# Three 256-column matmuls per weight block in the up groups of the MLPs, with ReLU and square on ScalarE

## The reference

```python
for i in range(DEPTH):                      # DEPTH = 2
    y = diff_attention(h, ...) if i % 2 == 0 else gla(h, ...)
    h = layer_norm(DN_ALPHA * h + y, ln_g[i, 0], ln_b[i, 0])
    f = squared_relu_mlp(h, mlp_w1[i], mlp_w2[i])
    h = layer_norm(DN_ALPHA * h + f, ln_g[i, 1], ln_b[i, 1])

def squared_relu_mlp(x, w1, w2):            # w1: 2048 x 8192, w2: 8192 x 2048
    return jnp.square(jax.nn.relu(x @ w1)) @ w2
```

## Time and profile before

| quantity | before |
|---|---|
| median of 3 runs | 2231.32 us |
| lowest, highest | 2231.12, 2233.16 us |
| span of the profiled execution, first to last instruction | 2231.0 us |
| TensorE (PE) busy | 99% of the span |
| VectorE (DVE), ScalarE (ACT) busy | 57%, 40% |
| mean granted TensorE clock | 0.997 of full speed |
| mean DMA rate | 187 GB/s |

### The profile page before, as it was taken

How to read it: one execution, slowest core, us unless ns; L and a number is a source line. 1 busy time by engine, 2 the same in 40 slices (tenths; PEclk the granted TensorE clock), 3 DMA queues, 4 the chain that set the end, 5 groups by cost and what they waited for, 6 DMA issues and landing times.

```text
span 2231.0 us, 28775 instructions
## 1 busy us (share of the span) xinstructions
PE 2208.7 (99%) x11312; PEld 1876.4 (84%) x11312; DVE 1262.0 (57%) x1074; ACT 897.8 (40%) x754; POOL 108.5 (5%) x94
## 2 busy tenths in 40 slices
PE   7999999999999999999999999999999999999998
PEld 6888888988888888888888888889888888888886
DVE  5555555854554464455676566668544645554555
ACT  4444443443343343343454344334434434433431
POOL 2000000300000000000020111102000000000000
PEclk9999999999999999999999999999999999999999
DMA  8545556654655554655446445647555546555542
GB/s 283 179 141 197 170 179 216 215 185 169 219 192 189 188 188 163 217 186 188 151 152 210 172 150 181 232 151 245 171 212 190 181 170 214 193 193 189 181 163 109
DMA packets 206592, 417.04 MB, mean 187 GB/s; under 512 B 6640, under 2 KB 6640, under 8 KB 205504
## 3 DMA queue, kind: packets, MB, share of 16 engines
q1 hardware_dynamic: 205056, 406.87, 53.4%
q0 software_dynamic: 1472, 9.25, 1.1%
HBM read 414.00 MB, written 2.10 MB: 187 GB/s over the span
## 4 chain that ended last, share of the span: by engine, by line
PE 98%; issue 0%; DMA 0%; DVE 0%; ACT 0%; POOLq 0%; POOL 0%; SPq 0%
PE ps L435 97%; PE ps L508 1%; DMA raw<-in_attn_w_qkv_dram 0%; PE ps L747 0%; PE ps L595 0%; DVE res L1233 0%; PE ps L576 0%; DVE res L1224 0%; ACT hi L782 0%; POOLq L89 0%; POOL ln_rstd L343 0%; SPq L291 0%; DVE ln_stats L1186 0%; DVE res L1060 0%; DVE ln_mean_var L1215 0%
## 5 line engine op out<-in xcount | busy, mean ns | idle before, releaser
L1040 DVE TENSOR_TENSOR lo<-raw,hi 128x2048 fp32r<-128x2048 f32 x384 | 882.0, 2303 | 582.9 <-ACT hi L782 582.8
L782 ACT ACTIVATE hi<-raw 128x2048 fp32r<-128x2048 f32 x384 | 734.5, 1917 | 929.4 <-PE ps L435 913.7
L435 PE MATMUL ps<-X,hi 128*128 128x512 f32 (+1 forms) x3008 | 994.3, 385 | 6.1 <-ACT hi L782 6.1
L435 PE MATMUL ps<-hi,F 128*128 128x512 f32 x2560 | 793.2, 390 | 0.0
L435 PE MATMUL ps<-X,lo 128*128 128x256 f32 x2816 | 769.5, 282 | 0.0
L435 PEld LDWEIGHTS ps<-X,hi 128*128 128x128 f32 x3008 | 553.4, 189 | 123.8 <-ACT hi L782 6.5
L435 PEld LDWEIGHTS ps<-hi,F 128*128 128x128 f32 x2560 | 480.5, 188 | 99.5
L435 PEld LDWEIGHTS ps<-X,lo 128*128 128x128 f32 x2816 | 530.1, 190 | 3.9
L435 PE MATMUL ps<-lo,F 128*128 128x512 f32 x1280 | 498.0, 389 | 0.0
L435 PEld LDWEIGHTS ps<-lo,F 128*128 128x128 f32 x1280 | 240.3, 188 | 49.5
L435 PE MATMUL ps<-hi,X 128*128 128x512 f32 x768 | 246.7, 396 | 0.0
(11 more groups left out here) (110 smaller groups left out, 528.0 us busy)
## 6 DMA issues: line engine op xcount, KB each, us to landing
raw<-in_mlp_w_dram SPq DMA_DIRECT2D x256, 1024.0 KB, 5.2
raw<-in_attn_w_qkv_dram SPq DMA_DIRECT2D x48, 1024.0 KB, 5.2
raw<-in_gla_w_in_dram SPq DMA_DIRECT2D x48, 1024.0 KB, 5.2
raw<-in_attn_w_o_dram SPq DMA_DIRECT2D x16, 1024.0 KB, 5.9
raw<-in_gla_w_o_dram SPq DMA_DIRECT2D x16, 1024.0 KB, 5.2
work<-in_ln_g_dram POOLq DMA_DIRECT2D x4, 1024.0 KB, 7.2
work<-in_ln_b_dram POOLq DMA_DIRECT2D x4, 1024.0 KB, 10.3
res<-in_x_dram SPq DMA_DIRECT2D x8, 256.0 KB, 11.1
```

The lines of the kernel that those rows point to most:

```text
L435: return pe.matmul(o, w, m, start=start, stop=stop)
L782: act.activation(hi[:, j], raw[:, j], ACT.Copy).then_inc(hi_ready, 1)
L1040: dve.tensor_tensor(lo[:, j], raw[:, j], hi[:, j].bitcast(F32), ALU.subtract).then_inc(lo_ready, 1)
```

## The change

In 15 of the 16 up groups of each MLP, `cols_group` is replaced by `up_group`. Each of the 64 weight blocks now gets three matmuls of 256 columns, all into one range of 256 PSUM columns: hi·X hi, hi·X lo, lo·X hi. The output blocks i share banks in pairs, so a group takes two banks (4·par and 4·par + 1) instead of four. Nothing is left to add: ScalarE reads both banks in one ReLU (128 x 1024), squares in place in a second instruction and later copies to F; VectorE only splits and writes the lo part of F, in one instruction of 1024 elements. There are two places for the hidden values, used in turn (`hidden`). The first up group of each MLP keeps `cols_by_block`, the copy and the add; it has windows of its own (`first_up_window`). Down groups, attention and GLA keep their instructions; some counters of `half_copied` change (`COPIED_MLP`, `COPIED_GLA`).

```diff
+        hidden = [part(5120, 4, SEQ), part(4096, 4, SEQ)]
@@ TensorE
-                    cols_group(g, 0, X)
+                    up_group(g, 0)
                 pe.wait_ge(res_added, 2 * r)
                 pe.wait_ge(halves_added, 2 * n)
-                cols_group(g + 1, 1, X)
+                up_group(g + 1, 1)
+
+            def up_group(g, par):
+
+                for j in range(TILES):
+                    pe.wait_ge(lo_ready, 4 * g + j + 1)
+                    for k in range(KPT):
+                        a = 4 * j + k
+                        first, last = a == 0, a == KT - 1
+                        for i in range(4):
+                            acc = ps[:, 4 * par + i // 2, (i % 2) * SEQ:(i % 2 + 1) * SEQ]
+                            mm(acc, hi[:, j, k, blk(i)], X[:, a, 0, :], first and i % 2 == 0, False)
+                            mm(acc, hi[:, j, k, blk(i)], X[:, a, 1, :], False, False)
+                            m = mm(acc, lo[:, j, k, blk(i)], X[:, a, 0, :], False, last and i % 2 == 1)
+                        if k == KPT - 1:
+                            m.then_inc(w_used, 1)
@@ ScalarE
+            def up_window(g, n, e, k, fk, hidden_free):
+
+                split_some(g + 1, 3)
+                act.wait_ge(w_used, 4 * g + 4)
+                act.wait_ge(*hidden_free)
+                act.activation(hidden[e].rearrange("p (b i) t -> p b (i t)", b=2), ps[:, 4 * e:4 * e + 2, :],
+                               ACT.Relu).then_inc(halves_added, 2)
+                act.wait_ge(halves_added, 2 * n + 2)
+                act.activation(hidden[e], hidden[e], ACT.Square).then_inc(squared, 2)
+                split_hi(g + 1, 3)
+                act.wait_ge(squared, k + 2)
+                act.activation(F[:, bass.ds(fk, 4), 0, :], hidden[e], ACT.Copy).then_inc(f_hi, 2)
...
@@ VectorE
+            def up_window(g, e, k, fk):
+                split_all(g + 1)
+                dve.wait_ge(f_hi, k + 2)
+                dve.tensor_tensor(F[:, bass.ds(fk, 4), 1, :], hidden[e], F[:, bass.ds(fk, 4), 0, :].bitcast(F32),
+                                  ALU.subtract).then_inc(f_lo, 2)
...
```

More of the change, by code:

```diff
@@ L74 @@
 COLS_GLA = 2 * PAIRS + 4 * CHUNKS
+COPIED_MLP = [2 * PAIRS, 2 * PAIRS + 5]
+COPIED_GLA = 2 * PAIRS + 1
 RES_MLP = [QUARTERS, 2 * QUARTERS + 4 * CHUNKS]
@@ L912, in _, with first_up_window @@
             ln_window(G_WO + 3, 1)
-            def up_window(g, n, par, k, fk):
+            def first_up_window(g, n, k):
                 split_some(g + 1, 3)
-                copy_halves(g, n, par, mlp_half)
+                copy_halves(g, n, 0, mlp_half)
                 split_hi(g + 1, 3)
@@ L921, in up_window @@
                     act.wait_ge(squared, k + (s + 1))
-                    act.activation(F[:, bass.ds(fk + 2 * s, 2), 0, :], mlp_hidden[:, s], ACT.Copy).then_inc(f_hi, 1)
+                    act.activation(F[:, 2 * s:2 * s + 2, 0, :], mlp_hidden[:, s], ACT.Copy).then_inc(f_hi, 1)
+            def up_window(g, n, e, k, fk, hidden_free):
[9 more added lines that the diff above has]
+                act.activation(F[:, bass.ds(fk, 4), 0, :], hidden[e], ACT.Copy).then_inc(f_hi, 2)
             def mlp(m, L):
                 g0, n0 = G_MLP[m], COLS_MLP[m]
-                with act.Fori(0, CHUNKS - 1) as ch:
+                k0 = 32 * m
+                first_up_window(g0, n0, k0)
+                up_window(g0 + 1, n0 + 1, 1, k0 + 2, 4, (halves_added, 2 * n0 + 2))
+                up_window(g0 + 2, n0 + 2, 0, k0 + 4, 8, (f_lo, k0 + 2))
+                up_window(g0 + 3, n0 + 3, 1, k0 + 6, 12, (f_lo, k0 + 4))
+                with act.Fori(0, 4) as q:
+                    split_all(q + (g0 + 5))
+                with act.Fori(1, CHUNKS - 1) as ch:
                     with act.Fori(0, 2) as p:
                         for e in range(2):
-                            up_window(8 * ch + 2 * p + (g0 + e), 4 * ch + 2 * p + (n0 + e), e,
-                                      8 * ch + 4 * p + (32 * m + 2 * e), 8 * p + 4 * e)
+                            k = 8 * ch + 4 * p + (k0 + 2 * e)
+                            up_window(8 * ch + 2 * p + (g0 + e), 4 * ch + 2 * p + (n0 + e), e, k, 8 * p + 4 * e,
+                                      (f_lo, k - 2))
                     with act.Fori(0, 4) as q:
@@ L935, in mlp @@
                     for e in range(2):
-                        up_window(2 * p + (g0 + e + 8 * ch), 2 * p + (n0 + e + 4 * ch), e,
-                                  4 * p + (32 * m + 2 * e + 8 * ch), 8 * p + 4 * e)
+                        k = 4 * p + (k0 + 2 * e + 8 * ch)
+                        up_window(2 * p + (g0 + e + 8 * ch), 2 * p + (n0 + e + 4 * ch), e, k, 8 * p + 4 * e,
+                                  (f_lo, k - 2))
                 with act.Fori(0, 3) as q:
@@ L1273, in _, with first_up_window @@
             ln_window(G_WO + 3, 3, ROWS_WO + 3, 1)
-            def up_window(g, n, par, k, fk):
+            def first_up_window(g, n, copied, k):
                 split_some(g + 1, 3)
-                dve.wait_ge(lo_ready, 4 * g + 7)
                 for s in range(2):
-                    dve.wait_ge(half_copied, 2 * n + (s + 1))
-                    b = 4 * par + 2 * s
+                    dve.wait_ge(half_copied, 2 * copied + (s + 1))
+                    b = 2 * s
                     dve.tensor_tensor(mlp_hidden[:, s], ps[:, b:b + 2, 0:SEQ], mlp_half[:, s], ALU.add
@@ L1290, in up_window @@
                     dve.wait_ge(f_hi, k + (s + 1))
-                    dve.tensor_tensor(F[:, bass.ds(fk + 2 * s, 2), 1, :], mlp_hidden[:, s],
-                                      F[:, bass.ds(fk + 2 * s, 2), 0, :].bitcast(F32), ALU.subtract
+                    dve.tensor_tensor(F[:, 2 * s:2 * s + 2, 1, :], mlp_hidden[:, s],
+                                      F[:, 2 * s:2 * s + 2, 0, :].bitcast(F32), ALU.subtract
                                       ).then_inc(f_lo, 1)
+            def up_window(g, e, k, fk):
[3 more added lines that the diff above has]
+                                  ALU.subtract).then_inc(f_lo, 2)
             def mlp(m, L):
                 g0, n0, r0, w0 = G_MLP[m], COLS_MLP[m], RES_MLP[m], ROWS_MLP[m]
-                with dve.Fori(0, CHUNKS - 1) as ch:
+                k0 = 32 * m
+                first_up_window(g0, COLS_MLP[m], COPIED_MLP[m], k0)
+                for u in range(1, 4):
+                    up_window(g0 + u, u % 2, k0 + 2 * u, 4 * u)
+                dve.wait_ge(res_scaled, 8 * (L + 1))
+                out_window(g0 + 4, 0, r0, w0, False, True, True)
+                with dve.Fori(1, QUARTERS) as q:
+                    out_window(q + (g0 + 4), q, q + r0, q + w0, False)
+                with dve.Fori(1, CHUNKS - 1) as ch:
                     with dve.Fori(0, 2) as p:
                         for e in range(2):
-                            up_window(8 * ch + 2 * p + (g0 + e), 4 * ch + 2 * p + (n0 + e), e,
-                                      8 * ch + 4 * p + (32 * m + 2 * e), 8 * p + 4 * e)
-                    dve.wait_ge(res_scaled, 8 * (L + 1))
+                            up_window(8 * ch + 2 * p + (g0 + e), e, 8 * ch + 4 * p + (k0 + 2 * e), 8 * p + 4 * e)
                     out_window(8 * ch + (g0 + 4), 0, 4 * ch + r0, 4 * ch + w0, False, True, True)
@@ L1308, in mlp @@
                     for e in range(2):
-                        up_window(2 * p + (g0 + e + 8 * ch), 2 * p + (n0 + e + 4 * ch), e,
-                                  4 * p + (32 * m + 2 * e + 8 * ch), 8 * p + 4 * e)
+                        up_window(2 * p + (g0 + e + 8 * ch), e, 4 * p + (k0 + 2 * e + 8 * ch), 8 * p + 4 * e)
                 out_window(g0 + 8 * ch + 4, 0, r0 + 4 * ch, w0 + 4 * ch, True, True, True)
@@ L1338, in gla_q @@
             def gla_q(u):
-                n = COLS_GLA + u
+                n, copied = COLS_GLA + u, COPIED_GLA + u
                 if u:
@@ L1343, in gla_q @@
                 for s in range(2):
-                    dve.wait_ge(half_copied, 2 * n + s + 1)
+                    dve.wait_ge(half_copied, 2 * copied + s + 1)
                     b = 4 * (u % 2) + 2 * s
@@ L1355, in gla_k_sums @@
             def gla_k_sums(u):
-                n = COLS_GLA + 2 + u
+                n, copied = COLS_GLA + 2 + u, COPIED_GLA + 2 + u
                 dve.wait_ge(q_ready, 4)
```

## The result

| | before | changed |
|---|---|---|
| median | 2231.22 us (4 runs, 2227.26 to 2233.16) | 2245.57 us (4 runs, 2244.02 to 2246.99) |
| span of the profiled execution | 2231.0 us | 2243.5 us |
| time against before | 1 | 1.0061, 95% interval 1.0049 to 1.0073 |

The change makes the kernel slower by 0.61%; the medians differ by 14.4 us. 2244.4 us were forecast, in a range of 2240.5 to 2258.0. The profiled spans differ by 12.5 us.

What follows compares the result with a forecast made beforehand. TensorE's matmul stream was taken to bound the kernel: 1920 blocks x (360.0 - 353.2) ns = +13.1 us on the 2231.0 us span gives 2244.1, plus 0.3 to the median, 2244.4 us; range 2240.5 to 2258.

Steps and rivals of the forecast that it cites:

- The bound: Whole kernel: TensorE is 99% busy and 98% of the chain, so only its stream of matmuls counts.
- The price of a block after: Changed up groups: three 256-column matmuls at 120.0 ns each, 360 ns per weight block instead of 353.2.
- The net of 6.8 ns: Per up-group block: 13.4 ns for one more matmul, less 6.6 ns of alignment loss that equal steps avoid.
- The sum and its cover: MLP up groups: 1920 blocks add 13.1 us; ScalarE's longer work stays hidden under over 10 us of cover.
- The prediction's step of 0.3 us from span to median: Whole kernel: the median lies 0.3 us above the profiled span, turning 2244.1 into 2244.4 us.
- The 3 us that the prediction allowed: Behind the GLA gate's small matmuls: the half-clock stretch may fall out or last longer, 3 us either way.
- (a): Changed up groups: alignment loss stays, a block takes 366.6 ns, +25.7 us, 2257.1 us; 14%.
- (b): Changed up groups: 256-column steps take 116.7 ns, a block 350.1 ns, -6.0 us, 2225.4 us; 6%.
- (c): Changed up groups: second use of the same hi block is nearly free, time stays 2231 to 2236.1 us; 5%.
- (d): TensorE in changed up groups: instruction feed or a new wait adds +7.7 to +21 us, 2252 to 2265; 8%.
- The rule of 2.5 ns: Any matmul step: columns / 2.4 + 2.5 ns, so the added matmuls cost +4.8 us, 2236.1 us.

Runs made afterwards that it cites:

- e3: Kernel before, with only the 512-column hi matmul of the up groups split into two of 256; 2245.2 us, 1.0060 of before.
- e7: Changed kernel with four more 128x1024 copies on ScalarE in each of the 30 up windows; 2245.33 us, 1.0066 of before.
- e2: Kernel before, with two throwaway 128x128 transposes ahead of each pair of up groups; 2228.78 us, 0.9991 of before.
- e5: Kernel before, 512-column matmul first in every up-group block, two throwaway transposes in the first block of each MLP chunk; 2226.36 us, 0.9982 of before.
- e8: Kernel before, 512-column matmul first in every up-group block, two throwaway transposes in the third block of each MLP chunk; 2226.12 us, 0.9973 of before.
- e9: Kernel before, 512-column matmul first in every up-group block, eight throwaway transposes in the third block of each MLP chunk; 2224.95 us, 0.9969 of before.
- e11: Kernel before, 512-column matmul first in every up-group block, four throwaway transposes in the third block of each MLP chunk; 2223.07 us, 0.9963 of before.
- e6: Changed kernel with the middle matmul of each block (hi x X lo) covering 128 columns instead of 256; 2225.03 us, one run.
- e4: Changed kernel with each block's matmuls ordered hi x X hi, lo x X hi, hi x X lo; 2246.05 us, 1.0066 of before.
- e1: Kernel before, with the 512-column matmul first in every block of every group of cols_group; 2232.19 us, 1.0004 of before.
- e10: Changed kernel with the middle matmul covering 128 columns and using only 32 of the block's 128 weight columns; 2212.29 us, one run.

## Why the prediction was right

**The bound.** TensorE's stream was all that counted: between e3 and the changed kernel VectorE's work differs by 74 us, and e7 adds some 130 us to ScalarE's, both without effect.

**The price of a block after.** 3 x 120.0 = 360 ns was forecast from the stretch with 256-column steps only the earlier trace rows; 92.14 / 256 = 359.9 was measured, in every changed group. The prediction took the steady 120.0 rather than the 119.7 of the short run, and that was right: 1.72 us per phase against the 1.74 of its sum.

**The net of 6.8 ns.** It was read as 13.4 for one more matmul less 6.6 for a lost alignment. The second part is shown by e2, e5, e8, e9 and e11: the pair runs at 347 or 353 ns in one and the same stage, with the same engines busy. The first part holds between 256 and 512 columns alone. Below 256 it does not: a step of 128 columns was to cost 66.7 ns by it, and in e6 it took 109. The prediction did not know this, and did not need it. Cutting the matmuls finer would have cost far more than 13.4 ns each: by an estimate from e6, two steps of 128 columns cost 2 x 109 = 218 ns in place of one of 120.

**The sum and its cover.** Predicted 13.1 us; the changed groups give 12.95 in the trace. The prediction also allowed for the three GLA groups to change their phase, at up to 1.3 us; two did, for 0.85 us (it read the short phase from one of them; the third was long already). Why they changed is open: their instructions are the same, and in the profiles of all other runs they are long too. ScalarE's timeline behind the same group as in the earlier trace rows:

```profile
604.26 1.03 ACT L947 ACTIVATE work<-ps 128x1024 f32<-128x1024 f32 x1 [4.04 <-PE ps L438]
605.38 1.06 ACT L950 ACTIVATE work<-work 128x1024 f32<-128x1024 f32 x1
606.34 1.90 ACT L800 ACTIVATE hi<-raw 128x2048 fp32r<-128x2048 f32 x1
608.15 1.04 ACT L953 ACTIVATE F<-work 128x1024 f32 x1
```

The group ends at 580.83 + 64 x 0.36 = 603.87; hi of tile 3 is there 4.4 us later (forecast 4.3), and nothing waits. No load of function tables was added: 3 in the whole kernel, as before. VectorE lost 74 us where 79 were forecast, ScalarE gained 27 where 29 were.

**The median.** It moved by 14.4 us where the span moved by 12.5. In every run for which both are on record, the time is 1.7 to 1.9 us more than the span (2245.27 and 2243.5 for the changed kernel). The span of 2231.0 thus belongs to an execution of about 2232.8 us, 1.6 above the median of the kernel before, and 1.51 of it was found above, ahead of the first MLP. The prediction's step of 0.3 us from span to median is the same as adding 13.1 us to the median, so it did no harm. That the median came within 1.2 us of the forecast is in part luck, since executions of one kernel lie 3 to 6 us apart; that the changed groups came within 0.15 us is not.

The half-speed stretch behind the gate's small matmuls is there in both profiles, in the changed one with a clock of 0.51:

```profile
1151.24:1157.00 5.76, 5.76 (x28) 5.76 (x28) 0.21 (x1) 5.60 (x10) 0.00 (x0) 0.51 0.56 182
```

It can be missing. The profile of e9 has none; its GLA stage, with all three groups long as in the changed kernel, takes 3.06 us less than the 303.55 there:

```profile
1111.23:1411.72 300.49, 300.49 (x1555) 251.50 (x1554) 190.41 (x159) 131.88 (x121) 44.91 (x32) 1.00 0.50 171
```

The 3 us that the prediction allowed for it are of the right size. Executions of the kernel before with a mean clock of 0.999, taken beside the experiments, took 2227.3 to 2231.0 us. The 2227.26 us among its four may be one of these (its clock is not on record); none of the changed kernel's four is.

**The rivals.** (a), a triple in a long phase, did not occur in any changed group. (b), steps of 116.7 ns, did not either: 120.0 throughout. (c), a repeated block for nothing, is refuted by e4, where steps cost the same without the repetition. (d): the waits of the weight loads for "issue" in the matmuls' line are unchanged:

```profile
PEld ps L438 <- issue: 6.4, 25, 0.7
```

The rule of 2.5 ns beyond the columns (the Trainium skill, "TensorE: Matmul & The Clock Gate", section "Back-to-back issue gap") would have put the kernel at 2236.1 us; the measured 2245.57 and the steps of 120.0 and 226.7 ns speak against it for matmuls of this type with a load each. The Trainium skill gives it in that section for a matmul by itself and says that a stream of loads and matmuls departs from it, so the prediction asked more of the rule than it states.

## What to carry to other kernels

Where TensorE bounds, price a rewrite of its matmuls by start-to-start distances in the trace, for each size and neighbourhood, and first look for a stretch that already has the new pattern: one such stretch gave this result to a tenth of a per cent. The same columns in more matmuls are slower, and work taken off an engine that nobody waits for is worth nothing. If a repeated pattern shows two different periods in one trace with all else equal, that difference may itself be a gain to be had: here 0.3 to 0.4%, about half of what the change lost, from eight or four throwaway transposes per chunk and a strict order. Such a gain must be read in every stretch of the trace: with two and with four transposes some stretches stayed long, and executions of one kernel differed by up to 13 us.

## What the runs showed of the hardware

- An alternating stream of 512- and 256-column matmuls, a weight load each, has two stable periods, 346.7 and 353.3 ns, with the same work of the other engines and nearly the same DMA rate beside it. The steps of the long one repeat after three blocks, 1.06 us. Strict alternation keeps either. Transposes between a 512 and a 256 can lead to the short one: at all three places in the attention stage (eight of them), in the profile of e9 (eight) and of e8 (two) at eight entries of eight, in that of e11 (four) at six, in that of e5 (two, two blocks earlier) at five. Eight transposes between a 256 and a 512 left the long one (e1). The turn of the order at a group's start threw the short one out (e2).
- Equal steps have one period: 120.0 ns for 256 columns, 226.7 ns for 512.
- Half the columns do not make half a step: with 128 instead of 256 streamed columns in one of three pairs of a load and a matmul, that pair takes 109 ns instead of 120, and the others stay at 119 and 121 (e6). With 32 instead of 128 weight columns in one load, the block of three loses 5.5 ns more (e10).
- The half-speed stretch behind the small matmuls of the GLA gate (clock 0.51 for 5.76 us) is in the profiles of the kernel before, the changed kernel and others, and not in that of e9; it is worth up to 3 us.
